# First attention: the gate blocks of a pair of steps in one group beside the short step

## The chip, the cores and the metric

One core of a Trainium2 chip runs the whole program. The metric is the device time of one launch in microseconds. The kernel before takes 792.78 us (median of 3 runs, 792.41 to 793.43).

## The reference, cut to what matters

The program is three transformer blocks in one launch: a differential attention block on 256 tokens and 256 context tokens, a grouped-query attention block, and a block with sparse attention, retention and a feed-forward part. The change touches only the attention of the first block:

```python
p = t @ w_in                                   # t: 256 tokens, and 256 context tokens
q, k, v, z = jnp.split(p, [...], axis=-1)      # 8 heads; q and k in two halves of 64, v of 128
o1 = sweep_attention(qq[..., 0, :], kk[..., 0, :], vv)    # softmax(q k^T) v
o2 = sweep_attention(qq[..., 1, :], kk[..., 1, :], vv)
o = o1 - lam * o2
o = rms_norm(o, subln_g) * (1.0 - lam_init)
y = (o * jax.nn.silu(gate)) @ w_out            # gate: the z columns of p
```

Tokens look at 512 keys (their own and the context's), context tokens at the 256 keys of the context.

## The kernel before, in words

All matrices are held with 128 partitions. There are four tiles of 128 rows: tiles 0 and 1 are the tokens, 2 and 3 the context. A product with weights is made of three fp32r matmuls per block of 128 input features (`gemm_unit`, lines 869 to 871): activation high part times weight high part, times weight low part, and low part times high part, 512 columns each. A unit is one tile times 512 output columns and has 8 such blocks (`k` 0 to 7). `FIRST` is `range(0, 4)`, `SECOND` is `range(4, 8)`.

Chunks 0 to 5 of the input projection `in0` (q, k, v) come first. The last two chunks, 6 and 7, are the gate `z`: 2 chunks x 4 tiles = 8 units = 64 blocks. They are not needed before the attention ends and are laid beside it.

The attention runs in 32 steps `p`. `STEPS0` alternates: an even step is a head of a token tile (512 keys, here the long step), an odd step a head of a context tile (256 keys, the short step). Each engine goes through its own list in order, and semaphores tie them:

- TensorE, per step: wait for the combined probabilities of `p`, transpose them (`turn_probs`, line 976; 4 transpositions in a long step, 2 in a short one); scores of step `p + 2` (`scores0`, line 1053; two halves of 64 rows, 3 matmuls each, of 512 or 256 columns); the gate blocks of this step (`gemm_unit`); wait for the copy of the transposed probabilities, then the values (`values0`, line 1078; 4 or 2 matmuls of 128 columns, and as many passes again). The probabilities are the stationary operand of the values, so their weight load reads the copy.
- ScalarE, per step: the exponentials of step `p + 1` (line 1579); `beside0(p - 1)`, a tanh of a gate unit if one was finished in step `p - 1` (line 1502); the square and the scaled copy of the output of step `p - 1` (`out0`, lines 1590 and 1498); the copy of the transposed probabilities of `p` from PSUM (line 1498, `sc<-psum`). Behind steps 4, 14, 18 and 30 it also rounds a half chunk of weights (line 1416).
- VectorE: the maximum of the scores (`max0`, line 2286), reciprocals and the combination of the two halves (`comb0`, line 2301), the product of the gate unit (`gate_z`, line 2308), and pieces of the low weight parts.

`BESIDE_ATTENTION0` (line 146) says which gate blocks go beside which step: before the change blocks 0; 1 to 3; 4; 5 to 7 beside the four steps of a unit, so one block in each long step and three in each short step. A unit ends in every fourth step (3, 7, ... 31), and its tanh comes in ScalarE's list of the long step behind it. Gate units take turns in PSUM banks 0 and 1 (`banks_plan`). The first half of a weight chunk is released by block 3 of its last tile, the second by block 7; both stay in the steps where they are.

Of the kernel before, what the change touches and what calls it, by code (L numbers as in the profile page):

```python
# [14 lines left out]
KT = D // P  # L15
XT = 2
NT = 4
# [4 lines left out]
HEADS = 8  # L22
# [13 lines left out]
FIRST, SECOND = range(HALF_KT), range(HALF_KT, KT)  # L36
# [79 lines left out]
def gemm_tiles(stage, chunk):  # L116
    if stage.startswith("ada"):
        return [0]
    if stage == "out0":
        return [0, 1, 2, 3] if chunk else TILES0  # L120
    if stage == "in0" or (stage, chunk) == ("in1", 2):
        return [0, 1, 2, 3]
    return [0, 1]
# [19 lines left out]
ASIDE = {("out1", 1, 1), ("in2", 1, 1), ("in2", 3, 1), ("out2", 0, 0), ("gu", 0, 0), ("down", 0, 0)}  # L143


BESIDE_ATTENTION0 = {p: (6 + p // 16, (p // 4) % NT, [range(0, 1), range(1, 4), range(4, 5), range(5, 8)][p % 4])
                     for p in range(NT * HEADS)}


SPLITS_BESIDE0 = [4, 14, 18, 30]  # L150
# [12 lines left out]
def banks_plan():  # L163
# [4 lines left out]
    def put(name, bank):  # L168
        place[name] = (bank, len(order[bank]))
        order[bank].append(name)  # L170
# [3 lines left out]
    def gemm_unit(stage, c, t):  # L174
        put((stage, c, t), turn[0] % 2)
        turn[0] += 1
# [37 lines left out]
                    put(("mod1", part), 7 - c % 2)  # L214
    for p in range(NT * HEADS):
        if p % HALF_KT == 0:
            gemm_unit("in0", *BESIDE_ATTENTION0[p][0:2])
        if p == 27:
            put(("turn_o0", 0, 0), 1)
            put(("turn_o0", 0, 1), 1)  # L220
        put(("s0", p, 0), 2 + 2 * (p % 2))
        put(("s0", p, 1), 3 + 2 * (p % 2))
        put(("t0", p), 6)
        put(("pv0", p), 7)
# [82 lines left out]
def block_kernel(nc, a, out):  # L307
    loads = loads_plan()
    load_no = {key: n for n, key in enumerate(loads)}
    halves = [key for key in loads if not key[0].startswith("ada")]  # L310
    half_no = {key: g for g, key in enumerate(halves)}
    place = banks_plan()

    ctx = ExitStack()
    with ctx:
# [194 lines left out]
        def half_width(key):  # L510
            stage, c, _ = key
            return IN2[c][1] if stage == "in2" else D if stage == "down" else COLS
# [5 lines left out]
        def lo_block(g, kk):  # L518
            return as_blocks(g, w_lo, load_no[halves[g]] % RAW)[:, kk, :]

        def hi_block(g, kk):

            if halves[g] not in ASIDE:
                return as_blocks(g, w_hi, slots[g])[:, kk, :]
            row = HALF_KT + 2 * (kk % 2)
            return (act_hi, act_lo)[kk // 2][:, row:row + 2, XT * P:]
# [194 lines left out]
        def bank_full(name):  # L721
            return full[place[name][0]]
# [9 lines left out]
        def moved(name):  # L732

            b, n = place[name]
            return free[b], n + 1

        def tile_cols(t, n=1):
            return slice(t * P, (t + n) * P)
# [82 lines left out]
        def _(pe):  # L821
            

            def begin(name):
                b, n = place[name]
                if n:
                    pe.wait_ge(free[b], n)
                return psum[:, b, :]

            def act_ready(stage, c, t, k):  # L830

                src = act_of[stage]
                if (stage, c, t) == ("in1", 2, XT):
                    pe.wait_ge(s_act, act_base["norm1c"] + k + 1)
                if c:
                    return
                if src == "norm0" and k < HALF_KT:
                    if t in (0, XT):
                        pe.wait_ge(s_lo0, HALF_KT * (t // XT) + k + 1)
                elif src in act_base:  # L840
                    if t == 0:
                        pe.wait_ge(s_act, act_base[src] + k + 1)
                elif k % HALF_KT == 0:
                    pe.wait_ge(*moved((src, t, k // HALF_KT)))

            def gemm_unit(stage, c, t, ks=range(KT)):

                name = (stage, c, t)
                o = psum[:, place[name][0], :] if ks[0] else begin(name)
                g0 = half_no[(stage, c, 0)]  # L850
                n = half_width(halves[g0])
                for k in ks:
                    h, kk = divmod(k, HALF_KT)
                    if kk == 0:
                        pe.wait_ge(s_wlo, g0 + h + 1)
                    hi, lo = hi_block(g0 + h, kk), lo_block(g0 + h, kk)
                    if stage == "in0" and c in BY_FEATURES:
                        pe.matmul(o, hi[:, tile_cols(t)], act_hi[:, k, :], start=(k == 0), stop=False)  # L858
                        pe.matmul(o, hi[:, tile_cols(t)], act_lo[:, k, :], start=False, stop=False)  # L859
                        mm = pe.matmul(o, lo[:, tile_cols(t)], act_hi[:, k, :], start=False, stop=(k == KT - 1))  # L860
                        if k == HALF_KT - 1 and t == NT - 1:
                            mm.then_inc(s_wused, 1)
                        elif k == KT - 1:
                            mm.then_inc(bank_full(name), 1)
                        continue
                    act_ready(stage, c, t, k)
                    x_hi, x_lo = act_hi[:, k, tile_cols(t)], act_lo[:, k, tile_cols(t)]
                    oh = o[:, 0:n].rearrange("p (a n) -> p a n", a=2) if len(hi.shape) == 3 else o[:, 0:n]
                    pe.matmul(oh, x_hi, hi, start=(k == 0), stop=False)  # L869
                    pe.matmul(o[:, 0:n], x_hi, lo, start=False, stop=False)  # L870
                    mm = pe.matmul(oh, x_lo, hi, start=False, stop=(k == KT - 1))  # L871
                    if k == HALF_KT - 1 and t == (gemm_tiles(stage, c)[-1] if stage != "gu" else XT - 1):
                        mm.then_inc(s_wused, 1)
                    elif k == KT - 1:
                        mm.then_inc(bank_full(name), 1)
# [97 lines left out]
            def turn_probs(name, src, blocks):  # L973
                o = begin(name)
                for i in range(blocks):
                    mm = pe.transpose(o[:, tile_cols(i)], src[:, tile_cols(i)], ident[:])  # L976
                mm.then_inc(bank_full(name), 1)
# [63 lines left out]
            def scores0(p):  # L1041
                t, h = STEPS0[p]
                keys = slice(0, NT * P) if t < XT else slice(XT * P, NT * P)
                n = keys.stop - keys.start
                o = [begin(("s0", p, s)) for s in range(2)]


                for i in range(3):
                    for s in range(2):
                        rows = slice(64 * s, 64 * s + 64)  # L1050
                        q = rest_q[rows, p, :] if i == 2 else round_q[rows, h, tile_cols(t)]
                        k = (rest_k if i == 1 else round_k)[rows, h, keys]
                        mm = pe.matmul(o[s][:, 0:n], q, k, start=(i == 0), stop=(i == 2))  # L1053
                        if i == 2:
                            mm.then_inc(bank_full(("s0", p, s)), 1)
# [26 lines left out]
            for p in range(NT * HEADS):  # L1082
                pe.wait_ge(s_comb, p + 1)
                turn_probs(("t0", p), sc[:, 4 + p % 2, :], XT if STEPS0[p][0] >= XT else NT)
                if p + 2 < NT * HEADS:
                    scores0(p + 2)
                c, t, ks = BESIDE_ATTENTION0[p]
                gemm_unit("in0", c, t, ks)
                if p in (0, 8):
                    for t in range(NT):  # L1090
                        pe.wait_ge(*moved(("in0", 5 * (p // 8), t)))
                values0(p)
                if p in (24, 26):
                    to_feature("turn_o0", [0], gate_units, parts=((p - 24) // 2,))
# [308 lines left out]
        def _(act):  # L1403
# [96 lines left out]
            def tanh_half(dst, name, n=COLS):  # L1500
                act.wait_ge(*finished(name))
                seq.note(act.activation(dst, psum[:, place[name][0], 0:n], ACTF.Tanh, scale=0.5).then_inc(s_tanh, 1), s_tanh)
# [90 lines left out]

            def beside0(p):

                c, t, ks = BESIDE_ATTENTION0[p]
                if ks[-1] == KT - 1:
                    tanh_half(gate_units[:, c - 6, t, :], ("in0", c, t))

            def last_in0(c, t):  # L1600
# [171 lines left out]
            for p in range(XT * HEADS):  # L1772
# [5 lines left out]
                if p % 4 == 3:  # L1778
                    c, t = z_units1[p // 4]
# [211 lines left out]
        def _(dve):  # L1991
# [335 lines left out]

            def beside0(p):

                c, t, ks = BESIDE_ATTENTION0[p]  # L2330
                if ks[-1] == KT - 1:
                    gate_z(gate_units[:, c - 6, t, :], ("in0", c, t))

            seq.note(dve.tensor_tensor(qkn2[:, 1, :], qkn2[:, 1, :], qkn2[:, 0, :], ALU.mult).then_inc(s_v, 1), s_v)
# [231 lines left out]
            for p in range(XT * HEADS):  # L2566
# [9 lines left out]
                if p in GATED_BESIDE1:  # L2576
                    c, t = GATED_BESIDE1[p]
# [408 lines left out]
```

## Time and profile before

| | before |
|---|---|
| median of 3 runs | 792.78 us |
| profiled execution | 792.75 us |
| span of the profiled execution | 790.8 us |
| mean granted TensorE clock | 0.996 |
| TensorE busy | 777.1 us (98%) |
| VectorE busy | 545.8 us (69%) |
| ScalarE busy | 394.7 us (50%) |
| first attention | about 184.6 to 292.6 us of the span |

The span runs from the first to the last instruction on the core; the time holds some 2 us more around it. "PE" is TensorE's matmuls, "PEld" its weight loads, "DVE" VectorE, "ACT" ScalarE. The ends of matmuls are modelled; consecutive matmuls overlap in the records, so that starts are what distances are read from.

### The profile page before, as it was taken

To read this page: it belongs to the slowest core of one execution; us is meant where nothing else is said; L and a number is where in the kernel's file an instruction comes from. 1 tells how busy PE (TensorE), PEld (TensorE's weight loads), DVE (VectorE), ACT (ScalarE), POOL (GpSimd) and SP (SyncE) were. 2 spreads that over 40 slices of the span, in tenths; PEclk is the share of its full clock that TensorE was granted. 3 is DMA by queue.
4 is the path that set the end of the run, shared out by engine and by line. 5 is a ranking of instruction groups with operands and counts; after the bars stand their busy time and mean duration, and the time that the engine had idled before them with its cause. 6 is when DMAs were issued, how large, how long until landed. Compare 5 with 4: busy or idle time off the path is not lost.

```text
span 790.8 us, 10917 instructions
## 1 busy us (share of the span) xinstructions
PE 777.1 (98%) x4012; PEld 620.1 (78%) x4012; DVE 545.8 (69%) x963; ACT 394.7 (50%) x742; POOL 42.3 (5%) x55
## 2 busy tenths in 40 slices
PE   8999999997999999999999999999999999999998
PEld 5578777885777787777888888787788888888886
DVE  3457987786768874779857667899878645465553
ACT  3552332325888773575657556735345434443431
POOL 1120000000001000112100002200010000000000
PEclk9999999998999999999999999999999999999999
DMA  9994554334000056339233035973216664566521
GB/s 336 389 342 159 213 212 140 114 110 169 2 2 1 1 190 236 107 107 338 114 107 107 1 110 174 381 253 107 80 55 213 223 203 160 172 213 201 188 78 54
DMA packets 71352, 125.76 MB, mean 159 GB/s; under 512 B 2714, under 2 KB 28652, under 8 KB 71172
## 3 DMA queue, kind: packets, MB, share of 16 engines
q1 hardware_dynamic: 70352, 123.00, 44.8%
q10 hardware_dynamic: 532, 1.21, 0.5%
q0 software_dynamic: 416, 0.85, 0.3%
q8 instruction: 33, 0.54, 0.3%
q14 instruction: 19, 0.16, 0.1%
HBM read 123.99 MB, written 1.06 MB: 158 GB/s over the span
## 4 chain that ended last, share of the span: by engine, by line
PE 83%; DVE 9%; ACT 3%; DMA 2%; issue 1%; POOL 1%; SPq 1%; DVEq 0%; ACTq 0%
PE psum L869 16%; PE psum L871 15%; PE psum L870 15%; PE psum L858 4%; PE psum L859 4%; PE psum L860 4%; PE psum L1078 3%; PE psum L1053 3%; PE psum L976 3%; PE psum L1379 3%; PE psum L1377 3%; PE psum L1378 3%; DVE w_lo L2001 2%; DMA act_lo_as_f<-in_ada_w 2%; PE psum L1151 2%; PE psum L891 2%
## 5 line engine op out<-in xcount | busy, mean ns | idle before, releaser
L870 PE MATMUL psum<-w_lo,act_hi 128*128 128x512 f32 (+1 forms) x624 | 242.3, 388 | 0.0
L869 PE MATMUL psum<-w_hi,act_hi 128*128 128x512 f32 (+1 forms) x584 | 238.0, 408 | 0.7 <-DVE act_lo L2177 0.4
L871 PE MATMUL psum<-w_hi,act_lo 128*128 128x512 f32 (+1 forms) x584 | 227.1, 389 | 0.0
L2001 DVE TENSOR_TENSOR w_lo<-raw,w_hi 128x2048 fp32r<-128x2048 f32 (+1 forms) x70 | 157.9, 2262 | 73.3 <-ACT w_hi L1416 73.2
L1416 ACT ACTIVATE w_hi<-raw 128x2048 fp32r<-128x2048 f32 (+1 forms) x74 | 139.9, 1895 | 68.7 <-PE psum L871 30.5
L869 PEld LDWEIGHTS psum<-w_hi,act_hi 128*128 128x128 f32 x584 | 109.8, 188 | 33.9 <-issue 11.8
L870 PEld LDWEIGHTS psum<-w_lo,act_hi 128*128 128x128 f32 x624 | 117.6, 188 | 20.9 <-issue 1.0
L871 PEld LDWEIGHTS psum<-w_hi,act_lo 128*128 128x128 f32 x584 | 109.8, 188 | 23.4
L1970 POOL TENSOR_TENSOR rstd<-ms,half_neg 128x1 f32<-128x1 f32 (+3 forms) x38 | 36.1, 951 | 545.8 <-DVE ms L2042 545.8
L858 PE MATMUL psum<-act_hi,w_hi 128*128 128x512 f32 x128 | 50.8, 397 | 0.0
L1579 ACT ACTIVATE sc<-psum,nmax 128x512 f32<-128x512 f32 (+1 forms) x64 | 36.8, 587 | 27.0 <-DVE nmax L2286 27.0
L859 PE MATMUL psum<-act_lo,w_hi 128*128 128x512 f32 x128 | 49.9, 390 | 0.0
L860 PE MATMUL psum<-act_hi,w_lo 128*128 128x512 f32 x128 | 49.9, 390 | 0.0
L1498 ACT ACTIVATE sc<-psum 128x512 f32<-128x512 f32 (+1 forms) x62 | 32.5, 526 | 14.7 <-PE psum L976 8.7
L2286 DVE TENSOR_REDUCE nmax<-psum 128x2 f32<-128x1024 f32 (+1 forms) x32 | 30.5, 955 | 12.1 <-PE psum L1053 12.0
L976 PE MATMUL psum<-ident,sc 128*128 128x128 f32 x184 | 30.2, 279 | 5.4 <-DVE sc L2301 4.4
L1378 PE MATMUL psum<-w_lo,act_hi 128*128 128x512 f32 x88 | 34.2, 389 | 0.0
L1925 ACT ACTIVATE sc<-psum 128x256 f32<-128x256 f32 x22 | 8.4, 383 | 50.6 <-PE psum L871 50.6
L1377 PE MATMUL psum<-w_hi,act_hi 128*128 128x512 f32 x80 | 31.2, 390 | 0.0
L1379 PE MATMUL psum<-w_hi,act_lo 128*128 128x512 f32 x80 | 31.1, 389 | 0.0
L858 PEld LDWEIGHTS psum<-act_hi,w_hi 128*128 128x128 f32 x128 | 24.0, 188 | 8.2 <-issue 3.4
L1078 PEld LDWEIGHTS psum<-vbuf,sc 128*128 128x128 f32 x192 | 27.1, 196 | 3.4 <-ACT sc L1498 0.6
(288 smaller groups left out, 1123.6 us busy)
## 6 DMA issues: line engine op xcount, KB each, us to landing
raw<-in_a_w_in SPq DMA_DIRECT2D x16, 1024.0 KB, 8.2
raw<-in_ada_w SPq DMA_DIRECT2D x14, 1024.0 KB, 5.4
raw<-in_w_out SPq DMA_DIRECT2D x12, 1024.0 KB, 5.3
raw<-in_w_gate SPq DMA_DIRECT2D x22, 512.0 KB, 4.1
raw<-in_w_up SPq DMA_DIRECT2D x22, 512.0 KB, 5.2
raw<-in_w_down SPq DMA_DIRECT2D x11, 1024.0 KB, 5.0
raw<-in_b_w_in SPq DMA_DIRECT2D x10, 1024.0 KB, 7.9
raw<-in_w_in SPq DMA_DIRECT2D x10, 1024.0 KB, 5.9
```

The lines of the kernel that those rows point to most:

```text
L858: pe.matmul(o, hi[:, tile_cols(t)], act_hi[:, k, :], start=(k == 0), stop=False)
L859: pe.matmul(o, hi[:, tile_cols(t)], act_lo[:, k, :], start=False, stop=False)
L860: mm = pe.matmul(o, lo[:, tile_cols(t)], act_hi[:, k, :], start=False, stop=(k == KT - 1))
L869: pe.matmul(oh, x_hi, hi, start=(k == 0), stop=False)
L870: pe.matmul(o[:, 0:n], x_hi, lo, start=False, stop=False)
L871: mm = pe.matmul(oh, x_lo, hi, start=False, stop=(k == KT - 1))
L976: mm = pe.transpose(o[:, tile_cols(i)], src[:, tile_cols(i)], ident[:])
L1377: pe.matmul(oh, x_hi, hi, start=(j == 0 and i == 0), stop=False)
L1378: pe.matmul(o, x_hi, lo, start=False, stop=False)
L1379: mm = pe.matmul(oh, x_lo, hi, start=False, stop=(last and i == 1))
L1416: ins = act.activation(hi, weights, ACTF.Copy)
L2001: ins = dve.tensor_tensor(rest, weights, hi.bitcast(F32), ALU.subtract)
```

## The change

The gate blocks of a pair of steps are issued in one group in the short step: blocks 0 to 3 or 4 to 7 of the unit. The long step issues none. `BESIDE_ATTENTION0` holds odd steps only, the bank plan looks the unit up at `p + 1`, and ScalarE's and VectorE's `beside0` act in the same steps as before. Everything else, the order included, is as it was.

```diff
-BESIDE_ATTENTION0 = {p: (6 + p // 16, (p // 4) % NT, [range(0, 1), range(1, 4), range(4, 5), range(5, 8)][p % 4])
-                     for p in range(NT * HEADS)}
+BESIDE_ATTENTION0 = {p: (6 + p // 16, (p // 4) % NT, SECOND if p % 4 == 3 else FIRST) for p in range(1, NT * HEADS, 2)}
...
         if p % HALF_KT == 0:
-            gemm_unit("in0", *BESIDE_ATTENTION0[p][0:2])
+            gemm_unit("in0", *BESIDE_ATTENTION0[p + 1][0:2])
...
                 if p + 2 < NT * HEADS:
                     scores0(p + 2)
-                c, t, ks = BESIDE_ATTENTION0[p]
-                gemm_unit("in0", c, t, ks)
+                if p in BESIDE_ATTENTION0:
+                    gemm_unit("in0", *BESIDE_ATTENTION0[p])
...
             def beside0(p):
 
-                c, t, ks = BESIDE_ATTENTION0[p]
-                if ks[-1] == KT - 1:
+                if p in BESIDE_ATTENTION0 and BESIDE_ATTENTION0[p][2] == SECOND:
+                    c, t, _ = BESIDE_ATTENTION0[p]
                     tanh_half(gate_units[:, c - 6, t, :], ("in0", c, t))
```

VectorE's `beside0` changes in the same way.

## Rows read from the trace of the kernel before

**Rows 1.** The page: busy time by engine, and the chain that ended last

```profile
PE 777.1 (98%) x4012; PEld 620.1 (78%) x4012; DVE 545.8 (69%) x963; ACT 394.7 (50%) x742; POOL 42.3 (5%) x55
...
PE 83%; DVE 9%; ACT 3%; DMA 2%; issue 1%; POOL 1%; SPq 1%; DVEq 0%; ACTq 0%
```

**Rows 2.** Table by stretches: start:end, length, busy per engine (instructions), PEclk granted clock

```profile
184.60:190.40 5.80, 5.74 (x21) 4.38 (x22) 4.26 (x6) 3.28 (x6) 0.00 (x0) 0.50 1.01 382
...
210.30:216.90 6.60, 6.60 (x45) 5.19 (x44) 5.33 (x10) 5.00 (x17) 0.00 (x0) 1.00 0.00 0
...
283.90:292.60 8.70, 8.54 (x53) 6.96 (x53) 5.81 (x13) 7.55 (x22) 0.00 (x0) 1.00 0.75 255
```

**Rows 3.** Waits from 184 to 293 us: us in total, times, longest

```profile
PE psum L976 <- DVE sc L2301: 4.4, 1, 4.4
...
PEld psum L1078 <- ACT sc L1498: 0.6, 1, 0.6
```

**Rows 4.** Timeline, TensorE, steps 8 to 10: start, us, engine, line, count

```profile
214.95 0.40 PE L1053 MATMUL psum<-round_k,rest_q 64*128 64x512 f32 x2
...
215.27 0.19 PEld L869 LDWEIGHTS psum<-w_hi,act_hi 128*128 128x128 f32 x1 [0.36 <-issue]
...
215.61 0.40 PE L870 MATMUL psum<-w_lo,act_hi 128*128 128x512 f32 x1
...
215.86 1.09 PEld L1078 LDWEIGHTS psum<-vbuf,sc 128*128 128x128 f32 x8
...
218.64 0.39 PE L869 MATMUL psum<-w_hi,act_hi 128*128 128x512 f32 x1
...
218.87 0.39 PE L870 MATMUL psum<-w_lo,act_hi 128*128 128x512 f32 x1
...
220.03 0.60 PE L1078 MATMUL psum<-vbuf,sc 128*128 128x128 f32 x4
...
220.47 0.60 PE L976 MATMUL psum<-ident,sc 128*128 128x128 f32 x4
```

**Rows 5.** Timeline, ScalarE and VectorE, steps 8 to 10

```profile
213.61 0.60 ACT L1502 ACTIVATE zbuf<-psum 128x512 f32<-128x512 f32 x1
...
214.91 0.60 ACT L1498 ACTIVATE sc<-psum 128x512 f32<-128x512 f32 x1
...
219.15 0.38 ACT L1498 ACTIVATE sc<-psum 128x256 f32<-128x256 f32 x1
219.16 0.75 DVE L2301 SCALAR_TENSOR_TENSOR sc<-sc,rinv 128x512 f32<-128x512 f32 x1
```

**Rows 6.** Timeline, ScalarE and weight loads, steps 10 and 16

```profile
220.67 0.37 ACT L1590 ACTIVATE vecs<-psum,rinv 128x128 f32<-128x128 f32 x1 [0.23 <-PE psum L1078]
...
221.28 0.60 ACT L1498 ACTIVATE sc<-psum 128x512 f32<-128x512 f32 x1
...
221.90 0.19 PEld L869 LDWEIGHTS psum<-w_hi,act_hi 128*128 128x128 f32 x1 [0.37 <-issue]
...
241.42 0.59 ACT L1498 ACTIVATE sc<-psum 128x512 f32<-128x512 f32 x1
...
241.70 0.19 PEld L869 LDWEIGHTS psum<-w_hi,act_hi 128*128 128x128 f32 x1 [0.36 <-issue]
```

**Rows 7.** Timeline, ScalarE and weight loads, steps 30 and 31

```profile
288.25 0.60 ACT L1498 ACTIVATE sc<-psum 128x512 f32<-128x512 f32 x1
...
288.90 0.97 PEld L1078 LDWEIGHTS psum<-vbuf,sc 128*128 128x128 f32 x8 [0.60 <-ACT sc L1498]
...
291.35 0.39 ACT L1498 ACTIVATE sc<-psum 128x256 f32<-128x256 f32 x1
```

**Rows 8.** Timeline, ScalarE and TensorE, step 0

```profile
186.31 0.61 ACT L1498 ACTIVATE sc<-psum 128x512 f32<-128x512 f32 x1
...
187.28 0.79 PE L869 MATMUL psum<-w_hi,act_hi 128*128 128x512 f32 x1
```

**Rows 9.** TensorE's own waits behind the attention, the first of five groups

```profile
PE psum L976 <- ACT sc L1880: 0.9, 2, 0.5
```

More of the change, by code:

```diff
@@ L2328, in beside0 @@
             def beside0(p):
-                c, t, ks = BESIDE_ATTENTION0[p]
-                if ks[-1] == KT - 1:
+                if p in BESIDE_ATTENTION0 and BESIDE_ATTENTION0[p][2] == SECOND:
+                    c, t, _ = BESIDE_ATTENTION0[p]
                     gate_z(gate_units[:, c - 6, t, :], ("in0", c, t))
```

## Prediction, made before the changed kernel ran

> **What bounds the kernel now.** I read the page first: TensorE is busy for 98% of the span and holds 83% of the chain that ended last [rows 1]. So a change that leaves TensorE's work as it is can win only where TensorE waits, and it loses wherever it makes TensorE wait. Next the table by stretches: the first attention runs from about 184.6 to 292.6 us, and a pair of steps takes 6.6 us in which TensorE is busy for 6.60; only the first stretch (granted clock 0.50, that is 1.2 GHz) and the last one (8.54 of 8.70) look different [rows 2]. Then the waits of this stage: apart from the 4.4 us before its first transposition, the weight loads of the values wait for 0.6 us, on a single one of ScalarE's 32 copies [rows 3]. There is hardly anything to win. What is left is to see how much cover the moved matmuls give, and for that I read the timeline of one pair, engine by engine.
>
> **What the change removes and adds.** Each gate block is three matmuls of 512 columns, about 0.23 us from start to start (218.64, 218.87 in [rows 4]), so 0.69 us a block. Of the 64 blocks, 16 leave the long steps (one each) and join the three of the following short step. No instruction is added or dropped, on any engine; the DMA issues, their order and the release of the weight buffers stay behind the same blocks (the fourth and the eighth of a unit). The sum of TensorE's work is 0.
>
> Switching costs neither. Leaving the half-height scores for a full-height matmul costs about 0.2 us: the last pair of score matmuls starts at 214.95 and should be through at 215.18, the next weight load starts at 215.27 and the second gate matmul at 215.61, 0.34 us behind the first instead of 0.23 [rows 4]. The long step has this switch before (scores, gate) and after (scores, values). I count 0; below I keep 0.11 us a step, one open weight load, as the bound to either side.
>
> **What stood behind the moved block.** In a long step TensorE transposes the probabilities, issues the scores of two steps later, then the gate block, then the values. The values read the copy that ScalarE makes of the transposed probabilities, so everything queued behind them on TensorE waits for that copy. Without the block TensorE stands at the values 0.8 us earlier than it does: where the gate's weight load now starts. So for every long step the question is whether the copy is through at the start of that load. The latency from the end of a copy to the weight load that waits for it is seen once: 288.25 + 0.60 = 288.85, load at 288.90, so 0.05 us [rows 7].
>
> Step 8 (with a tanh): the copy runs 214.91 + 0.60 = 215.51 [rows 5]; TensorE will be there at 215.27 [rows 4]. It waits 0.24 + 0.05 = 0.29 us. The copy is late because ScalarE must first do the tanh of the finished gate unit (213.61, 0.60), then the square and the scaled copy of the short step before. This is the case of every second long step, 4, 8, ... 28.
> Step 10 (no tanh): copy until 221.28 + 0.60 = 221.88, TensorE there at 221.90 [rows 6]: 0.03 us.
> Step 16: copy until 241.42 + 0.59 = 242.01, load at 241.70: 0.36 us [rows 6].
>
> I read the two rows of each of the 14 steps from 2 to 28; these three are shown. Copy end minus load start is 0.23, 0.24, 0.23, 0.31, 0.31, 0.23, 0.31 in the seven steps with a tanh, and -0.02, 0.04, -0.02, -0.02, -0.02, -0.03, 0.07 in the others. With 0.05 us each: 1.86 + 0.35 = 2.21 and 0.00 + 0.35 = 0.35, together 2.56 us.
>
> Do these waits shrink later ones? In step 10 ScalarE sat idle for 0.23 us until the short step's values ended [rows 6]: it follows TensorE, so when TensorE comes late, so does the copy. In step 8 the tanh starts at 213.61 with no idle of ScalarE before it [rows 5], so there ScalarE's own queue may be the later one; but the long step before it, without a tanh, has put TensorE off by only 0.02 to 0.12 us, and that is all the relief there can be. I take none.
>
> Step 0 runs at half clock. TensorE would be at its values at 187.28, the copy ended at 186.31 + 0.61 = 186.92 [rows 8]: no wait. The block goes to step 1; the work until the clock rises is as dense as before.
>
> Steps 30 and 31: there are no scores left to issue, so the gate block of step 30 is the only cover, and even with it the load of the values waits 0.60 us, until 288.90 [rows 7]. Taking the block out leaves the values at 288.90, because the copy doesn't move. The block is then paid in step 31, where nothing hides it: the copy of that step ends at 291.35 + 0.39 = 291.74 [rows 7] and TensorE doesn't wait for it even with three blocks (the one wait of [rows 3] is that of step 30). 3 x 0.23 = 0.69 us.
>
> The short step has cover for all this: in step 9 the copy ends at 219.15 + 0.38 = 219.53 and the values start at 220.03 [rows 4, 5]. The long combination ends at 219.16 + 0.75 = 219.91, 0.56 us before its transposition at 220.47; four blocks and the same values lie between its scores and this point before and after, so its room doesn't change.
>
> **Sum.** 2.56 + 0.69 = 3.25 us longer. Behind the attention TensorE waits six times, 2.1 us in all, the costliest group 0.9 us in two waits [rows 9]; each is for a ScalarE or VectorE step that itself follows TensorE, none for a transfer, so nothing takes the delay back. The profiled execution took 792.75 us (span 790.8, 1.95 around it), as good as the median of 792.78: I forecast 796.0.
>
> **Rivals.**
> A (forecast): +3.25, 796.0; 70%.
> B: the waits don't repeat. If the copies of the tanh steps hang on ScalarE's own queue and not on TensorE, TensorE falls behind once, by about 0.3, and finds later copies done: 0.3 + 0.69 = +1.0, 793.8. For it: the tanh starts at once behind the exponential, and the steps with 0.31 are those whose ScalarE queue is later. Against it: the 0.23 us of idle in step 10, where ScalarE waits for TensorE [rows 6]. 14%.
> C: the first weight load of the values costs extra. It now starts at 215.86, under the last gate matmul, and is free [rows 4]; behind a wait it is open. I hold that it is the same 0.11 us that the gate pays after the scores; if both stand, 15 x 0.11 = 1.65 more: +4.9, 797.7. 7%.
> The Trainium skill, "TensorE: Matmul & The Clock Gate", section "Step-by-step: what each phase is for", says that TensorE pulls weight loads ahead of running matmuls; the load at 215.86 agrees [rows 4]. By that rule the load that was hidden under the gate matmul is lost as cover and C would hold, +4.9; by the row the load behind the scores starts only when they are through, gate or not, and +3.25 stands.
> D (the other side, not slower): the clock. The stage opens with 5.8 us at 0.50, 1.2 GHz, so 2.9 us are lost [rows 2], behind 4.4 us of idle TensorE [rows 3]. The change alters what TensorE runs there (values and a transposition come where the block was). Should the clock rise sooner for it, each us sooner wins 0.5. Only near the very start, -2.9, would the change come out even: +0.3, 793.1; it decides from a rise before about 186. Against it: TensorE is busy without a gap in this stretch, before and after. 5%.
> The same page, section "What's actually happening", has activity release the clock; the trace agrees as far as the low clock follows the idle time [rows 2, 3]. By that rule an equally active stretch keeps its rise where it is, and D wins nothing: +3.25.
> Something I don't see, to either side: 4%.
>
> **Numbers.** What a measurement of this kernel can tell from no change is 0.2%, 1.6 us: slower means above 794.4. A, C and a third of B's spread give 0.80; the rest of B and most of D, 0.15; faster 0.05. For A alone: latency 0 instead of 0.05 takes 0.7 off, and relief another 0.4; 0.11 us in half of the steps adds 0.8: 794.9 to 796.8. For 8 in 10 I widen towards B and C: 793.9 to 797.4.
>
> **What would show it.** After: in the long steps with a tanh the values' weight load is idle for 0.2 to 0.4 us with ScalarE's copy as what ended it, in the others below 0.1; the waits of TensorE's loads on that copy in the stage grow from 0.6 us; a pair takes 6.75 us in the mean instead of 6.6; step 31 begins its values 0.69 us later against its transposition. The stages behind are shifted and otherwise the same. I am wrong if the copies end before TensorE asks for them, or if the stage gets no longer than 0.7 us.

## The result and the profile after

The changed kernel takes 795.76 us (median of 7 runs, 794.62 to 796.46), the kernel before, run beside it, 792.77 us (7 runs, 791.96 to 793.56): a ratio of 1.004, 95% interval 1.003 to 1.005, so about 3.0 us slower. The forecast was 796.0, in the range 793.9 to 797.4. The profiled execution took 795.35 us (span 793.3), 2.60 us more than that of before. Some runs of either kernel are 0.5 to 1 us apart by the moment at which the clock rises in the first pair (below), so medians of few runs scatter by that much, and one run of e6 below, at 1971.72 us beside 805.45 to 806.58, is left out of its ratio.

The page of the changed kernel, busy time and the waits from 184 to 296 us (they answer to [rows 1] and [rows 3]; `L1077` is the values' line, before 1078; the columns are us in total, times, longest):

```profile
PE 776.6 (98%) x4012; PEld 619.3 (78%) x4012; DVE 545.8 (69%) x963; ACT 394.5 (50%) x742; POOL 42.3 (5%) x55
```

```profile
PEld psum L1077 <- ACT sc L1497: 8.0, 14, 1.1
...
PE psum L975 <- DVE sc L2300: 4.4, 1, 4.4
PE psum L1077 <- ACT sc L1497: 2.7, 8, 0.9
```

The busy time and the counts are those of before. What is new is the wait of the values' weight loads for ScalarE's copy: 14 times instead of once (step 30 and 13 of the 14 steps from 2 to 28; step 8 stands apart, see the last section).

The timeline of the changed kernel, ScalarE and weight loads, steps 10, 12 and 16 (they answer to [rows 5] and [rows 6]):

```profile
220.94 0.37 ACT L1589 ACTIVATE vecs<-psum,rinv 128x128 f32<-128x128 f32 x1 [0.65 <-PE psum L1077]
...
221.54 0.60 ACT L1497 ACTIVATE sc<-psum 128x512 f32<-128x512 f32 x1
...
222.19 0.97 PEld L1077 LDWEIGHTS psum<-vbuf,sc 128*128 128x128 f32 x8 [0.41 <-ACT sc L1497]
...
228.44 0.60 ACT L1497 ACTIVATE sc<-psum 128x512 f32<-128x512 f32 x1
...
229.09 0.52 PEld L1077 LDWEIGHTS psum<-vbuf,sc 128*128 128x128 f32 x4 [0.65 <-ACT sc L1497]
...
242.01 0.59 ACT L1497 ACTIVATE sc<-psum 128x512 f32<-128x512 f32 x1
...
242.66 0.86 PEld L1077 LDWEIGHTS psum<-vbuf,sc 128*128 128x128 f32 x7 [0.70 <-ACT sc L1497]
```

The load starts 0.05 to 0.06 us behind the end of the copy in each of them. A load behind the scores has 0.36 us of idle time without any wait [rows 4]; what is above that is the wait: 0.05 us in step 10 (no tanh), 0.29 in step 12 (tanh), 0.34 in step 16 (tanh, ScalarE late).

Steps 30 and 31 (they answer to [rows 7]):

```profile
290.10 0.59 ACT L1497 ACTIVATE sc<-psum 128x512 f32<-128x512 f32 x1
...
290.75 0.97 PEld L1077 LDWEIGHTS psum<-vbuf,sc 128*128 128x128 f32 x8 [1.09 <-ACT sc L1497]
...
293.19 0.38 ACT L1497 ACTIVATE sc<-psum 128x256 f32<-128x256 f32 x1
...
294.50 0.64 PEld L1077 LDWEIGHTS psum<-vbuf,sc 128*128 128x128 f32 x4
```

From the load of step 30 to that of step 31 it is 3.75 us, before 288.90 to 291.97, 3.07 us. Idle time in front of step 30's load has grown from 0.60 to 1.09 us.

The table by stretches for the first pair and the rest of the stage, the kernel before and then the changed one (it answers to [rows 2]; the first row of before stands there):

```profile
190.40:293.00 102.60, 102.44 (x653) 81.17 (x652) 76.30 (x154) 81.18 (x256) 3.31 (x2) 1.00 0.07 24
```

```profile
184.60:190.40 5.80, 5.72 (x27) 4.28 (x28) 4.28 (x6) 3.28 (x6) 0.00 (x0) 0.58 1.02 384
190.40:293.00 102.60, 99.90 (x631) 78.75 (x631) 74.66 (x153) 79.92 (x254) 3.31 (x2) 1.00 0.06 22
```

TensorE's busy time in the 102.6 us falls by 2.54 us. In the first stretch the granted clock is 0.58 instead of 0.50: it rose near 189.5 us instead of 190.7. The stage can be laid side by side by the starts of its transpositions and of the last values' load. The transpositions of steps 2 and 28, before and then changed:

```profile
194.05 0.60 PE L976 MATMUL psum<-ident,sc 128*128 128x128 f32 x4
...
280.82 0.60 PE L976 MATMUL psum<-ident,sc 128*128 128x128 f32 x4
```

```profile
193.54 0.60 PE L975 MATMUL psum<-ident,sc 128*128 128x128 f32 x4
...
282.34 0.60 PE L975 MATMUL psum<-ident,sc 128*128 128x128 f32 x4
```

Distances in us, from the profiled execution of each kernel (the experiments follow below):

| | step 0 to 2 | 2 to 28 | 28 to 30 | 30 to the values of 31 |
|---|---|---|---|---|
| before | 9.39 | 86.77 | 6.62 | 4.53 |
| changed | 8.86 | 88.80 | 6.95 | 5.21 |
| e1, last pair only | 8.14 | 86.75 | 6.62 | 5.20 |
| e2, all but the last pair | 8.26 | 88.55 | 6.90 | 4.53 |
| e3, tanh behind the copy | 8.87 | 87.53 | 6.63 | 5.21 |
| e4, two and two | 9.12 | 89.87 | 6.85 | 4.22 |
| e7, both costs undone | 8.89 | 87.66 | 6.63 | 4.52 |

The changed kernel's three later parts are 2.03 + 0.33 + 0.68 = 3.04 us longer. The first part is 0.53 us shorter, but it also varies by over 1 us between kernels that are the same there (before and e1), with the moment of the clock's rise (190.7 us before, near 188.0 in e1). Behind the attention the waits are those of before (0.9 us in two waits on the costliest, as in [rows 9]).

### The profile page after: what moved, and what is told of

Read it like the earlier page. It is cut to its first block, busy times and chain, and to the rows that moved or that the text cites. A ratio compares the mean times of both kernels' runs of the same rounds, so it can differ in the third digit from the quotient of the medians.

```text
span 793.3 us, 10917 instructions
## 1 busy us (share of the span) xinstructions
PE 776.6 (98%) x4012; PEld 619.3 (78%) x4012; DVE 545.8 (69%) x963; ACT 394.5 (50%) x742; POOL 42.3 (5%) x55
## 4 chain that ended last, share of the span: by engine, by line
PE 78%; DVE 10%; ACT 7%; DMA 2%; issue 2%; POOL 1%; SPq 1%; DVEq 0%; ACTq 0%
PE psum L868 15%; PE psum L870 14%; PE psum L869 14%; PE psum L857 4%; PE psum L858 4%; PE psum L859 4%; PE psum L1378 3%; PE psum L1377 3%; PE psum L1376 3%; DVE w_lo L2000 2%; PE psum L1077 2%; PE psum L975 2%; DMA act_lo_as_f<-in_ada_w 2%; PE psum L1150 2%; ACT sc L1578 2%
## 5 line engine op out<-in xcount | busy, mean ns | idle before, releaser
L1077 PEld LDWEIGHTS psum<-vbuf,sc 128*128 128x128 f32 x192 | 25.9, 196 | 10.7 <-ACT sc L1497 8.0
L1077 PE MATMUL psum<-vbuf,sc 128*128 128x128 f32 x192 | 29.1, 289 | 2.7 <-ACT sc L1497 2.7
```

Source lines behind the costliest of these rows:

```text
L1077: mm = pe.matmul(o[:, 0:P], probs[:, tile_cols(i)], vbuf[:, NT - blocks + i, tile_cols(h)], start=(i == 0), stop=(i == blocks - 1))
```

## The experiments

Two theories stood against each other. Cover: the moved block gave ScalarE the time for its copy, and without it TensorE waits. Regrouping: TensorE itself pays for the new order (a weight load that no running matmul hides, called open here, or the switch between half-height and full-height matmuls).

Where the table of a kernel is changed so that a step has no gate block, TensorE, ScalarE and VectorE skip it there; these lines are left out of the cuts of code below.

**Undoing or doing a part.** e1 groups the last pair only, e2 all pairs but the last.

```diff
 # e1, on the kernel before
+BESIDE_ATTENTION0[30] = (7, 3, range(0))
+BESIDE_ATTENTION0[31] = (7, 3, SECOND)
 # e2, on the kernel before
+for p in range(0, NT * HEADS - 2, 2):
+    BESIDE_ATTENTION0[p] = (*BESIDE_ATTENTION0[p][0:2], range(0))
+    BESIDE_ATTENTION0[p + 1] = (*BESIDE_ATTENTION0[p][0:2], FIRST if p % 4 == 0 else SECOND)
```

> The kernel before, with the gate blocks grouped in the last pair only (none in step 30, four in step 31). Cover theory (the change costs because the values of a long step reach ScalarE's copy too early): the block of step 30 stood in a wait that is there anyway and is now paid in step 31, +0.69 us, 793.5 against 792.8; nothing else moves. Rival, regrouping itself costs (an open weight load or a mode switch per pair): one pair of 16, +0.2 us at most.

> The changed kernel with the last pair as it was before (one block in step 30, three in 31). Cover theory: the full change less 0.69, so +1.9 to +2.6 against before, 795.0. Rival, the loss sits at the end of the stage: nearly all of +3.0 goes and about 793 is left.

Measured: e1 792.90 us against 792.60 of before beside it, ratio 1.0002 (0.9993 to 1.0011); e2 794.95 us, 1.0030 (1.0019 to 1.0040), +2.4 us. The interval of e1 holds both 0 and 0.69, so the time alone doesn't settle it; its trace does: the last part is 5.20 instead of 4.53 us, +0.67, and the 13 pairs ahead of it are unchanged (86.75 and 86.77). e2 is the mirror: 88.55 in the middle, 4.53 at the end. The two costs are separate.

**Taking away what makes the copy late.** e3 is the changed kernel with ScalarE's tanh behind the copy in six of the seven long steps (not in step 24, where a transposition waits for the bank), and VectorE's product one step later.

```diff
-                if p:
-                    beside0(p - 1)
+                if p == 24:
+                    beside0(p - 1)
+                if p:
                     out0(p - 1)
                 n = XT * P if STEPS0[p][0] >= XT else NT * P
                 move(sc[:, 6 + p % 2, 0:n], ("t0", p), n=n, wait_for=("pv0", p - 2) if p >= 2 else None)
+                if p and p != 24:
+                    beside0(p - 1)
...
-                beside0(p - 1)
+                if p == 24:
+                    beside0(p - 1)
+                elif p % 2 and p != 25:
+                    beside0(p - 2)
```

> The changed kernel, but in six of the seven long steps with a tanh ScalarE does the copy of the probabilities first and the tanh behind it, and VectorE the gate product one step later, behind its maximum. Cover theory: the waits of these six steps fall from about 0.3 to about 0.05 us each, 1.5 to 1.8 us less than the changed kernel, +1.2 to +1.5 against before (794.2). Rival, regrouping itself costs on TensorE whatever ScalarE does: the time stays at about +3.

Measured: 793.37 us against 792.60, ratio 1.0013 (1.0004 to 1.0022), +0.8 us by the medians and 0.3 to 1.7 by the interval. The median flatters e3: 6 of its 11 runs have a mean clock of 0.998, but only 6 of the 25 of the kernel before. Run against run at the same clock it is +1.3 us (793.23 against 791.96 at 0.998) to +1.5 (three runs at 0.996, 794.42, against 792.87), and its trace gives +1.45 in the three later parts. The middle part falls from 88.80 to 87.53 us and step 28 to 30 from 6.95 to 6.63. The trace of e3 around step 8, and the copy and the load of step 12:

```profile
214.70 0.60 ACT L1497 ACTIVATE sc<-psum 128x512 f32<-128x512 f32 x1
...
215.18 0.60 ACT L1501 ACTIVATE zbuf<-psum 128x512 f32<-128x512 f32 x1
...
228.09 0.60 ACT L1497 ACTIVATE sc<-psum 128x512 f32<-128x512 f32 x1
...
228.73 0.97 PEld L1077 LDWEIGHTS psum<-vbuf,sc 128*128 128x128 f32 x8 [0.40 <-ACT sc L1497]
```

In steps 4, 12, 16, 20 and 28, all with a tanh, the load now has 0.40 us of idle time, as in the steps without. TensorE's order is that of the changed kernel, instruction for instruction, so most of the loss was not TensorE's own: the rival falls.

**Both undone.** e7 is e3 with the last pair as before.

> The changed grouping with both of its costs taken away at once: the last pair as before (one block in step 30, three in 31), and in six of the seven long steps with a tanh the copy ahead of the tanh. Cover theory: e3_tanh_behind (+0.8 by medians, +1.3 to +1.5 at equal clock) less 0.5 to 0.7 for the last pair, so 0 to +0.8 against before, 793.0; what is left are the short waits of 0.03 to 0.1 us and those of steps 5 and 6. Rival, the two are one and the same loss seen twice: no gain on e3_tanh_behind.

Measured: 793.67 us against 793.09, ratio 1.0013 (1.0004 to 1.0022), +0.6 us. By the medians e7 can't be told from e3; at the same clock it is +0.5 us (793.80 against 793.29 at 0.996) to +1.0 (794.09 against 793.09, the latter from two runs only, at 0.995), less than e3's +1.3 to +1.5. By the traces the last part falls from 5.21 to 4.52 us, and the middle one stays 0.89 us longer than before: what is left of the change with both large costs undone is a loss, made of the 0.04 us waits, of step 24, and of steps 5, 6 and 8.

**The other direction.** e4 gives the long step more cover: two blocks in each step.

```diff
-... [range(0, 1), range(1, 4), range(4, 5), range(5, 8)][p % 4])
+... [range(0, 2), range(2, 4), range(4, 6), range(6, 8)][p % 4])
```

> The kernel before with the blocks dealt two to the long and two to the short step. Cover theory: the long step has more cover than it needs, and the short step's copy is measured against its long neighbour's exponentials, with the same blocks before it; 0.0 to -0.3 us (the second block of step 30 fills its wait, step 31 then waits for its copy). Rival, the short step needs its three blocks as cover: its copy would be late by 0.69 - 0.45 = 0.24 us in 16 steps, +3.8 us.

Measured: 795.46 us, ratio 1.0032 (1.0020 to 1.0045), +2.9 us. My expectation was wrong. The loss is nearer to the rival's +3.8, but with another cause than the one it named: the values never wait here. The waits of e4 and the timeline of VectorE and the weight loads around step 10:

```profile
PEld psum L976 <- DVE sc L2301: 7.9, 16, 4.8
```

```profile
219.08 0.69 DVE L2286 TENSOR_REDUCE nmax<-psum 128x2 f32<-128x512 f32 x1 [1.86 <-PE psum L1053]
...
220.19 0.75 DVE L2301 SCALAR_TENSOR_TENSOR sc<-sc,rinv 128x512 f32<-128x512 f32 x1
...
221.00 0.42 PEld L976 LDWEIGHTS psum<-ident,sc 128*128 128x128 f32 x4 [0.21 <-DVE sc L2301]
```

The long step's transposition waits for VectorE's combination in 15 steps, 3.1 us in all beside the 4.8 of step 0. The combination stands in VectorE's list behind the maximum of the short step's scores, and a second block in the long step makes those scores 0.7 us later. Before, that maximum was already the last thing the combination followed, but there was room:

```profile
218.05 0.69 DVE L2286 TENSOR_REDUCE nmax<-psum 128x2 f32<-128x512 f32 x1 [1.08 <-PE psum L1053]
```

It ended at 218.74 (218.05 + 0.69), the combination at 219.91, and the transposition came 0.56 us later, at 220.47 [rows 4, 5]. A block of 0.69 us is 0.13 us more than this room, and the wait is 0.21 us (0.06 of it from the end of the combination, 220.94, to the load at 221.00). The 0.56 us stood in my prediction; I did not hold it against this block. So the block counts on both sides: taken out of the long step it leaves the copy too little time, put into it it makes the combination late.

**A dose.** ScalarE copies the long step's probabilities twice.

```diff
+                if p % 2 == 0:
+                    ...
+                    seq.note(act.activation(sc[:, 6, 0:n], psum[:, place[("t0", p)][0], 0:n], ACTF.Copy).then_inc(s_a, 1), s_a)
+                    act.wait_ge(*seq.last)
                 move(sc[:, 6 + p % 2, 0:n], ("t0", p), n=n, ...)
```

> The kernel before, with ScalarE doing the copy of a long step's probabilities twice, one behind the other (a dose of about 0.62 us per long step). Cover theory: before the change the copy ends 0.26 us ahead of the values' first weight load in the steps with a tanh and 0.6 us ahead in the others, so the dose comes through at about 0.2 us in 7 steps, hardly in the other 7, and in full in step 30: +2 us, with what falls on the steps beside a weight split up to +3.5. Rival, ScalarE is off TensorE's path in this stage either way: 0.6 us or less.

> The changed kernel with the same second copy in each long step. Cover theory: nothing stands between scores and values, so the dose comes through in full in 14 steps and in step 30: 15 x 0.62 = 9.3 us on top of the changed kernel's +3, so +12 against before. Rival, regrouping costs on TensorE itself and the copy has slack: the same difference as between the two kernels without the second copy, +5 to +6.

Measured: e5 ratio 1.0053 (1.0038 to 1.0068), +4.2 us; e6 1.0173 (1.0158 to 1.0189), +13.7 us (both by the ratio). The waits of e5, and those of e6, over the whole stage:

```profile
PEld psum L1078 <- ACT sc L1498: 5.8, 11, 1.2
```

```profile
PEld psum L1077 <- ACT sc L1497: 16.7, 14, 1.7
```

With the same dose the changed kernel loses 13.7 - 3.0 = 10.7 us, the kernel before 4.2: the block absorbs over half of it. e5 is 2.2 us above my +2 and 0.7 above its upper bound of +3.5, e6 is 1.7 above my +12; where these come from is open.

**Where there was something to win.** TensorE waits for 4.4 us ahead of step 0, and then runs at 1.2 GHz for 5.8 us [rows 2, 3]. f1 issues blocks 0 to 2 of the first gate unit there; f2 also puts VectorE's maximum of step 2 ahead of a weight split; f3 fills the rest of the gap with matmuls whose result isn't used; f4 cuts the split in two; f5 deals two and two in the last pair only. Each contains the one before it.

```diff
 # f1
+BESIDE_ATTENTION0[0] = (6, 0, range(3, 4))
+BESIDE_ATTENTION0[1] = (6, 0, range(0))
+            gemm_unit("in0", 6, 0, ks=range(0, 3))      # ahead of step 0
 # f2
+            max0(2)
             split_through(half_no[("in0", 6, 1)])
-            max0(2)
 # f3
+            for _ in range(10):
+                pe.matmul(o, act_hi[:, 0, 0:P], act_hi[:, 0, :], start=True, stop=True)
 # f4: split_piece(0) in place of that split, split_piece(1) behind the combination of step 2
 # f5
+BESIDE_ATTENTION0[30] = (7, 3, range(4, 6))
+BESIDE_ATTENTION0[31] = (7, 3, range(6, 8))
```

> The kernel before, with blocks 0 to 2 of the first gate unit issued ahead of step 0, in the 4.4 us in which TensorE waits for the first combination; step 0 keeps block 3, step 1 has none. Theory: TensorE has 2.07 us less to do behind step 0 and an idle time of 2.3 us instead of 4.4, after which the clock may stay at 2.4 GHz; but the copy of step 1 is bound by VectorE's weight split ahead of its maximum (copy end 191.97), so step 2 starts at about 192.5 instead of 194.05: -1.5 us, 791.1. Rival, TensorE's work isn't what bounds the first pair: no change, 792.6.

> As f1_fill, and VectorE takes the maximum of step 2 ahead of the weight split. Theory: the exponentials of step 2 start 2 us sooner, the combination of step 2 ends near 191.4, and step 2 starts there instead of at 194.05: -2.5 us, 790.1, if the clock stays up in the first pair; -1 if it falls all the same, since then TensorE needs until about 193. Rival, as for f1_fill: 792.6.

> As f2_fill_max_first, and the 2.3 us of idle time that are left ahead of step 0 are filled with 10 matmuls whose result is not used (they write a PSUM bank that the first transposition overwrites). Theory: the granted clock stays at 2.4 GHz through the first pair, the scores of step 2 end about 0.6 us sooner, and the chain maximum, split, maximum, combination starts from there: step 2 begins at about 191.4 instead of 192.3, -0.9 us on f2, 790.0. Rival, the clock falls all the same or the chain on VectorE is bound elsewhere: 791.

> As f3, with VectorE's weight split (2.29 us) cut into two pieces, one ahead of the maximum of step 3 and one behind the combination of step 2. Theory: the combination of step 2 ends 1.1 us sooner, near 190.2, and -1.0 us more than f3, 789.0. Rival: the second piece makes the combination of step 3 and the maximum of step 4 late by as much, 790.

> As f4, with two gate blocks in step 30 and two in step 31 instead of one and three. Cover theory: step 30 waits 0.6 us for its copy in the kernel before, so a second block there is nearly free; step 31 is shorter by 0.69 until its own copy (291.74) holds it: -0.2 to -0.4 us on f4. Rival, from the run with two and two in all pairs: no gain, the copy of step 31 takes it all back.

Measured, each against the kernel before beside it: f1 1.0004 (0.9995 to 1.0013); f2 0.9981 (0.9972 to 0.9990), 790.98 us; f3 0.9985 (0.9976 to 0.9994), 791.01; f4 0.9970 (0.9958 to 0.9981), 790.11; f5 0.9967 (0.9955 to 0.9980), 789.84 against 792.55. f2 to f5 beat both kernels; f5 by 2.6 us. f4 and f3, and f5 and f4, can't be told apart by their intervals; f3 and f4 both stay about 1 us behind what I had expected (790.0 and 789.0). In f5's trace the part from step 30 to the last values takes 4.35 us instead of f4's 4.53.

f1 won nothing in the median: TensorE's waits only moved, as the expectation had it for the copy of step 1, and in 8 of its 11 runs the clock fell all the same. The other three, with a mean clock of 0.999 or 1.000, took 791.17 to 791.64 us, near the expected 791.1. The table by stretches of the profiled f1:

```profile
184.00:185.00 1.00, 0.01 (x1) 0.01 (x1) 0.96 (x3) 1.00 (x4) 0.00 (x0) 1.00 1.04 408
185.00:186.00 1.00, 1.00 (x8) 0.79 (x10) 0.77 (x3) 1.00 (x1) 0.00 (x0) 1.00 1.06 412
186.00:187.00 1.00, 1.00 (x7) 0.36 (x4) 0.68 (x1) 1.00 (x3) 0.00 (x0) 0.54 1.04 406
187.00:188.00 1.00, 1.00 (x3) 0.81 (x4) 1.00 (x1) 0.26 (x1) 0.00 (x0) 0.50 1.05 385
```

In f3 it stayed up in the profiled execution (mean clock 1.000, as in 5 of its 11 runs), and the waits of TensorE from 180 to 195 us (f2, then f3) show why that alone brought nothing that can be measured:

```profile
PE psum L978 <- DVE sc L2306: 3.4, 2, 2.3
PE psum L1082 <- ACT sc L1503: 0.3, 1, 0.3
```

```profile
PE psum L1085 <- ACT sc L1506: 1.1, 1, 1.1
PE psum L978 <- DVE sc L2309: 0.7, 1, 0.7
```

The faster TensorE waits longer for the copy of step 1. (Of f2's 3.4 us, 2.3 are the gap ahead of step 0.) Step 2 starts at 192.31 in f2, 0.9 us behind my figure: its combination stands behind the maximum of step 3, which had to wait for TensorE's scores.

## Why the prediction was right

- **Nothing to win, all to lose by waits.** Right. The other stages and the busy times are unchanged, and none of e1 to e7 came out faster than the kernel before.
- **Switching and open weight loads cost 0.** Right within what can be seen. The load stands 0.36 us behind the scores in both kernels, and e3 takes most of the loss away with TensorE's order untouched: what is left in its middle part, 0.76 us, is less than 14 open loads of 0.11 us (1.54). Rival C, +4.9, falls.
- **Waits of the steps with a tanh.** I had 0.28 to 0.36 us, 2.21 in all; the loads show 0.29 or 0.34 in six of the seven. Only step 8 is larger, 0.45 (below), and the seven add up to 2.34.
- **Waits of the others.** 0.35 us in all was forecast. The loads show 0.04 to 0.05 in each, 0.29 in the seven; in steps 6 and 26, where I had 0.09 and 0.12, the copy followed TensorE more closely.
- **The waits repeat.** Right, B falls: 14 waits, not one. In step 10 ScalarE's idle time for TensorE has grown from 0.23 to 0.65 us, so the copy does follow.
- **Step 30.** 0.69 forecast, 0.68 in the changed kernel, 0.67 in e1.
- **The sum.** 2.56 + 0.69 = 3.25 forecast. The parts of the table give 3.04; the waits read off the loads of steps 2 to 28 add up to 2.63 where the distances give 2.36, so moving the block seems to save about 0.02 us per pair by itself. From transposition to transposition a long step without a tanh shrinks from 3.11 us to 2.45 with a wait of 0.04 in it, so by 0.70, and the short step grows from 3.49 to 4.18, so by 0.69. I had put this term at 0; why it isn't was not tested. The forecast is as close as it is because the waits came out 0.07 us above it and this term 0.27 below.
- **Rival D.** The clock rose about 1.2 us sooner in the profiled execution of the changed kernel, worth the 0.53 us of the first part. But e1, which is the kernel before in this stretch, gained more (8.14), and so the change isn't its cause. The 3.04 less this is 2.51 us; the spans of the two profiled executions differ by 2.5, their times by 2.60.

## What to carry to other kernels

A block of work that looks idle-free in its place can be cover for another engine's chain: before moving it, read for each instruction behind it when its operand was ready and when its engine would arrive without the block; the two rows per step gave each wait here to within 0.1 us but for one. Then ask the same for what the block will stand in front of in its new place: e4 lost as much as the change by a maximum that came 0.7 us later. Where TensorE is busy for 98%, look for the single large gap (4.4 us here) and for the other engines' order around it, not for another deal of the same work.

## What the runs showed that I had not expected

- Step 8 waits longer than its copy explains: its load has 0.81 us of idle time (the fence below) and starts at 215.57, the copy ended at 215.35 (214.75 + 0.60), 0.22 us instead of the 0.05 of the other steps, and 0.22 and 0.21 in e3 and e7. Steps 0 and 8 are those where TensorE's list has four more waits, for values that were long in place, between the scores and the values, and step 0 runs at the lower clock. With the gate block ahead of them they cost nothing that can be seen. That they are the cause is argued, not tested.

```profile
215.57 0.97 PEld L1077 LDWEIGHTS psum<-vbuf,sc 128*128 128x128 f32 x8 [0.81 <-issue]
```

- After 2.3 us without a matmul the granted clock still fell from 1.00 to 0.50 in f1, and it did so over a microsecond after the work had begun again (1.00 in 185 to 186 us, 0.54 in the next). In the same execution it fell a second time, near 192.9 us, behind TensorE's new gap of 1.7 us in step 1 (190.65 to 192.36), and stayed at 0.50 until about 196.3. In the profiled f4, the slowest of its six runs (791.48 us), it fell near 191.8 us, behind a gap of 1.1 us (188.96 to 190.08). The profiled f3 has a gap of 1.1 us in the same place and kept its clock. So a change that fills one gap can lose by the next, and not in every run.
- Two executions of one kernel can differ by 0.5 to 1 us by when the clock comes back: in the first batch the 6 runs of the kernel before with a mean clock of 0.998 average 791.96 us, the 18 with 0.996 average 792.87 us.
